# Seven products of halves for eight in 18 of 22 projection steps, and the splits of their weights on ScalarE and VectorE

## What is computed

```python
h    = rms_norm(x, norm_w)
proj = h @ w_in                       # 1024 x 1024 times 1024 x (all columns)
gq, gk, gv, g_low, gr, hq, hf, hi, hg, sz, sxbc, sdt, gates = split(proj)
...                                   # GLA, HGRN2 and Mamba-2 (conv over sxbc) give y, 2048 wide
x2   = x + merged(y, sigmoid(gates)) @ w_out
h2   = rms_norm(x2); route each token to 1 of 4 groups, 2 of 8 experts
out  = rms_norm(x2 + w1 * expert1(h2) + w2 * expert2(h2), final_w)
```

## Time and profile before

| | us |
|---|---|
| median of 3 runs | 2144.92 (2144.08 to 2148.81) |
| the profiled execution | 2143.66 |
| its span, first to last instruction | 2142.0 |
| mean granted TensorE clock | 0.971 of full speed |
| project, from its first product to the next block's first | 139.07 to 628.17 |
| mixers, from there to the merge's first product | 628.17 to 1163.89 |

### The profile page before, as it was taken

The page is one execution under the profiler, slowest core; times in us unless marked ns, Lnnn a source line. Parts: engine busy times, 40 slices in busy tenths (PEclk is TensorE's granted clock), DMA queues, the critical chain, the costliest instruction groups (busy, mean ns, idle before and its releaser), DMA issues. The chain is left out here.

```text
span 2142.0 us, 26814 instructions
## 1 busy us (share of the span) xinstructions
PE 1979.7 (92%) x10826; PEld 1621.3 (76%) x10827; DVE 1337.7 (62%) x1475; ACT 921.4 (43%) x998; POOL 362.7 (17%) x203
## 2 busy tenths in 40 slices
PE   6999999999999999999997999986699999999994
PEld 5778888888987777777775787865588888888872
DVE  5930000576215777877874565556698999999974
ACT  4211010112114444444443334231578888878863
POOL 4223232243310000000001000012122222222210
PEclk9999999999999999999998999998799999999997
DMA  5242222224236553565645754451799999999986
GB/s 160 82 157 98 99 98 79 78 79 137 80 103 151 151 165 120 147 157 161 149 121 187 258 216 162 154 206 60 293 367 382 386 391 384 388 386 388 386 328 247
DMA packets 217236, 435.97 MB, mean 204 GB/s; under 512 B 27730, under 2 KB 150754, under 8 KB 189602
## 3 DMA queue, kind: packets, MB, share of 16 engines
q1 hardware_dynamic: 185954, 361.97, 49.3%
q10 hardware_dynamic: 20288, 51.39, 6.7%
q0 software_dynamic: 10880, 21.03, 2.6%
HBM read 369.67 MB, written 81.43 MB: 211 GB/s over the span
## 5 line engine op out<-in xcount | busy, mean ns | idle before, releaser
L636 DVE TENSOR_SCALAR tap<-u,taps 128x1024 f32<-128x1024 f32 x16 | 20.1, 1297 | 293.1 <-ACT u L594 293.1
L666 PE MATMUL ps<-h_hi,w_hi 128*128 128x512 f32 x576 | 178.1, 391 | 2.4 <-PEq L58 2.4
L666 PE MATMUL ps<-h_hi,w_lo 128*128 128x512 f32 x576 | 177.8, 390 | 0.0
L666 PE MATMUL ps<-h_lo,w_hi 128*128 128x512 f32 x576 | 177.7, 390 | 0.0
L2416 DVE TENSOR_TENSOR gu_lo<-gate_raw,gu_hi 128x2048 fp32r<-128x2048 f32 x64 | 146.6, 2293 | 32.8 <-ACT gu_hi L2361 32.7
L1311 PE MATMUL psum<-h_hi,l_hi 128*128 128x512 f32 x384 | 158.7, 413 | 3.5 <-PEq L58 3.5
L1311 PE MATMUL psum<-h_lo,l_hi 128*128 128x512 f32 x384 | 160.1, 417 | 0.0
L1311 PE MATMUL psum<-h_hi,l_lo 128*128 128x512 f32 x384 | 157.5, 410 | 0.0
L2416 DVE TENSOR_TENSOR gu_lo<-up_raw,gu_hi 128x2048 fp32r<-128x2048 f32 x64 | 146.4, 2287 | 13.7 <-ACT gu_hi L2361 13.7
L2421 DVE TENSOR_TENSOR dn_lo<-dn_raw,dn_hi 128x2048 fp32r<-128x2048 f32 x62 | 142.0, 2292 | 16.4 <-ACT dn_hi L2371 13.2
L604 ACT ACTIVATE out<-ps 128x2048 f32<-128x2048 f32 x14 | 26.4, 1883 | 270.2 <-PE ps L666 201.2
(11 more groups left out here) (383 smaller groups left out, 4863.2 us busy)
## 6 DMA issues: line engine op xcount, KB each, us to landing
gate_raw<-moe SPq DMA_DIRECT2D x66, 1024.0 KB, 8.4
up_raw<-moe SPq DMA_DIRECT2D x64, 1024.0 KB, 8.1
dn_raw<-moe SPq DMA_DIRECT2D x62, 1024.0 KB, 7.5
w_raw<-w_in SPq DMA_DIRECT2D x26, 1024.0 KB, 6.3
dn_raw<-w_br SPq DMA_DIRECT2D x15, 1024.0 KB, 7.4
l_raw<-w_gates ACTq DMA_DIRECT2D x24, 512.0 KB, 6.0
s_gates<-l_out ACTq DMA_DIRECT2D x48, 256.0 KB, 4.4
gate<-s_gates SPq DMA_DIRECT2D x16, 768.0 KB, 5.6
```

What stands on the lines that cost most here:

```text
L666: ins = nc.tensor.matmul(ps[b][:, a * T + half * 512:a * T + half * 512 + 512], w[:, k, a * P:(a + 1) * P], h[:, k, half * 512:half * 512 ...
```

## The change

1. **project** runs as two tokens steps, then 18 row steps with silu and conv in turn (the last two are silu), then two tokens steps, unrolled. A row step has 7 groups of 12 matmuls of 512 columns (Strassen's scheme in Winograd's form, one level, over halves of the columns, of k and of the tokens). The tokens' sums of halves `th`, `tl` are built once at the start of the block on DVE and ACT. The weights' sums of halves (`summed`), the subtractions of the splits (`lower`) and three additions of results (`added`) are on DVE, the casts (`upper`) and copies out of PSUM on ACT; POOL has only the two tiles of the gates left. The first tap of a convolution moves to ACT. PE waits for ACT's copies before groups 2 and 4 and for DVE's addition before group 6, since they use the same PSUM banks again. Outputs go out as two transfers a step. `out[0]` is the gates' `l_raw`, so these are loaded at the end of the block.
2. **norm1_and_decays**: the transposes of chunks 1 and 3 go to a second PSUM tile, the casts of chunks 2 and 3 to ACT, chunk 4 is transposed after PE's first products have begun.
3. **ident** is built in each stage that uses it; in the mixers POOL builds it last.
4. `gates` and `y` are laid out in DRAM so that each partition reads 4 to 6 KB in a row.
5. **merge_and_route**: the work beside the second half comes one column tile later, DVE's order at its end changes, the records' constant fields are written ahead, the last places come before the last `h2`, the records are read before `work` is stored; this block and the experts' end without a drain of POOL.
6. **finish**: `ON_PE` is (2, 3, 5, 6).

```diff
 norm1_and_decays, ScalarE and TensorE
+                if c == NCH // 2:
+                    upper_part(2)
+                    upper_part(3)
...
-            TURNS = {(0, 4): NCH // 2 + 1, (1, 2): NCH // 2 + 2, (2, 0): NCH // 2 + 3}
+            TURNS = {(0, 2): NCH // 2, (0, 7): NCH // 2 + 1, (1, 4): NCH // 2 + 2, (2, 1): NCH // 2 + 3}
 project, ScalarE
+            def step(n):
+                b, before = n % 2, is_conv(n - 1)
+                act.wait_ge(group_done, G * n + 1)
...
+                nc.scalar.copy(place(n, 0, 0), X[b]).then_inc(snap_ready, 1)
+                upper(n + 1, 0)
+                act.wait_ge(group_done, G * n + 2)
+                nc.scalar.copy(place(n, 1, 1), Y[b]).then_inc(snap_ready, 1)
+                upper(n + 1, 1)
+                act.wait_ge(group_done, G * n + 3)
+                nc.scalar.copy(place(n, 0, 1), X[b]).then_inc(snap_ready, 1)
+                for g in (2, 3, 4):
+                    upper(n + 1, g)
+                if before:
+                    conv_out(n - 1, 0)
+                upper(n + 1, 5)
+                if not is_conv(n):
+                    act.wait_ge(c_ready, 3 * n + 3)
+                    nc.scalar.activation(row(n, 0), row(n, 0), ACT.Silu).then_inc(out_ready, 1)
+                    send(n, 0)
+                act.wait_ge(group_done, G * n + 7)
...
+                upper(n + 1, 6)
+                if is_conv(n):
+                    conv_first(n, 0)
+                    conv_first(n, 1)
+                else:
+                    nc.scalar.activation(place(n, 1, 1), place(n, 1, 1), ACT.Silu).then_inc(out_ready, 1)
+                    act.wait_ge(x_read, n + 1)
+                    send(n, 1)
+                if before:
+                    conv_out(n - 1, 1)
...
+            for n in range(N):
+                step(n)
+            tokens_hi(N + HEAD, 2)
+            act.wait_ge(c_ready, 3 * N)
+            tokens_hi(N + HEAD + 1, 3)
+            tokens_out(N + HEAD, 2)
 project, VectorE
+            def step(n):
+                m = n + 1
+                summed(m, 0)
+                tap(n - 1, 0, 1)
+                lower(m, 0)
+                tap(n - 1, 0, 2)
+                lower(m, 1)
+                summed(m, 1)
+                tap(n - 1, 0, 3)
+                lower(m, 2)
+                summed(m, 2)
+                tap(n - 1, 1, 1)
+                added(n, 0)
+                lower(m, 3)
+                tap(n - 1, 1, 2)
+                added(n, 1)
+                summed(m, 3)
+                lower(m, 4)
+                tap(n - 1, 1, 3)
+                added(n, 2)
+                lower(m, 5)
+                lower(m, 6)
 project, TensorE
+            def step(n):
+                b = n % 2
+                moving = (rows_of(0, 0), (th[0], tl[0]), (th[1], tl[1]), rows_of(1, 0), (th[2], tl[2]), rows_of(1, 1), (th[3], tl[3]))
+                for g, (bank, first) in enumerate(((X, True), (Y, True), (X, False), (Z, True), (X, False), (Y, False), (X, False))):
+                    pe.wait_ge(split_ready, G * n + g + 1)
...
+                    if g == 2:
+                        pe.wait_ge(snap_ready, 3 * n + 1)
+                    if g == 4:
+                        pe.wait_ge(snap_ready, 3 * n + 3)
+                    if g == 6:
+                        pe.wait_ge(c_ready, 3 * n + 2)
 mixers, GpSimd, VectorE and TensorE
             nc.gpsimd.memset(mean_b[:], 1.0 / 256).then_inc(const_ready, 1)
+            nc.gpsimd.memset(ident[:], 0.0).then_inc(ident0, 1)
+            pool.wait_ge(ident0, 1)
+            nc.gpsimd.affine_select(out=ident[:], in_=ident[:], compare_op=ALU.not_equal, fill=1.0, base=0,
+                                    pattern=[[-1, P]], channel_multiplier=1).then_inc(ident_ready, 1)
...
             dve.wait_ge(mask_ready, NL)
+            dve.wait_ge(ident_ready, 1)
...
             pe.wait_ge(tok_loaded, 32)
+            pe.wait_ge(ident_ready, 1)
 merge_and_route
-        block = ctx.enter_context(nc.Block())
+        block = ctx.enter_context(nc.Block(no_gpsimd_drain=True))
...
+    def beside(n):
+
+        return 2 <= n - DM < 2 + HC
...
             for n in range(DM, 2 * DM):
-                gated(n)
+                if n < 2 * DM - 1:
+                    gated(n)
                 rest_w(step_of(n) + 2)
...
+            gated(2 * DM - 1)
+            pick_second(0)
+            weights(0)
...
+            weights(3)
+            places(3)
             h2(HC + 3, 5)
-            places(3)
 finish
-    ON_PE = (1, 3, 4, 6)
+    ON_PE = (2, 3, 5, 6)
 the tensors in DRAM
-        ("gates", [3072, T], F32),
+        ("gates", [2, D // P, P, 3, T // 2], F32),
...
-        ("y", [2048, T], F32),
+        ("y", [2, P, 16, T // 2], F32),
```

More of the change, by code:

```diff
@@ L510, in project @@
         sem = semaphores(nc, ctx, qk_stored)
[L511 to L514, removed]
+        whole = lambda ap: ap.rearrange("p b k n -> p (b k n)")
+        tiled = lambda ap: whole(ap).rearrange("p (k t) -> p k t", t=S)
+        out = [whole(l_raw), sb("out1", [P, 2 * T])[:]]
+        th = [sb(f"th{i}", [P, KH, S], F32R) for i in range(3)] + [tiled(l_hi)]
@@ L529, in project, with block_of @@
         block = ctx.enter_context(nc.Block())
[L531 to L545, removed]
+        def block_of(n, i, j):
+            return w_raw[:, n % 2, j * KH:(j + 1) * KH, i * P:(i + 1) * P]
@@ new lines, in tap @@
+            def tap(n, a, k):
+                if not is_conv(n):
+                    return
+                if k == 1:
+                    dve.wait_ge(tap_ready, 2 * convs(n) + a + 1)
+                    if a == 0:
+                        dve.wait_ge(c_ready, 3 * n + 3)
+                    else:
+                        dve.wait_ge(x_read, n + 1)
+                ins = nc.vector.scalar_tensor_tensor(row(n, a), u[a][:, k:k + T], tap_col(n, a, k), row(n, a),
+                                                     ALU.mult, ALU.add)
+                if k < SSM_CONV - 1:
+                    own.link(ins)
+                else:
+                    ins.then_inc(conv_ready, 1)
@@ new lines, in _ @@
+            for b in range(2):
+                dve.wait_ge(qk_stored[b], 16 * 2)
+            rows(0)
+            tokens_split(1, 0)
+            rows_split(0)
+            for k in range(1, KH):
+                rows(k)
+                rows_split(k)
+            for a in range(2):
+                nc.vector.memset(u[a][:, 0:PAD], 0.0).then_inc(pad_ready, 1)
+            dve.wait_ge(pad_ready, 2)
+            summed(0, 0)
+            lower(0, 0)
+            lower(0, 1)
+            summed(0, 1)
@@ L670, in _, with tokens @@
-            steps(pe, body)
+            def tokens(t, i):
+                b = t % 2
+                if i:
+                    pe.wait_ge(tok_split, i)
+                if i >= 2:
+                    pe.wait_ge(x_read, N - 3 + i)
+                    pe.wait_ge(c_ready, 3 * (N - 3 + i))
+                parts = ((w_hi[:, b], h_hi), (w_hi[:, b], h_lo), (w_lo[:, b], h_hi))
+                for c in range(NCH):
+                    for k in range(KT):
+                        for n, (w, h) in enumerate(parts):
+                            ins = nc.tensor.matmul(ps[b][:, c * PAIR:(c + 1) * PAIR], h[:, k, c * CH:(c + 1) * CH], w[:, k, :],
+                                                   start=k == 0 and n == 0, stop=k == KT - 1 and n == 2)
+                ins.then_inc(tok_done, 1)
@@ L673 @@
+            tokens(0, 0)
+            tokens(1, 1)
+            for n in range(N):
+                step(n)
+            tokens(N + HEAD, 2)
+            tokens(N + HEAD + 1, 3)
 LATE_T = WIDTHS["gates"] // P
```

491 lines of the change are left out of this document (317 added, 174 removed).

## The result

The changed kernel takes 2125.1 us (median of 4 runs, 2123.06 to 2130.35), the kernel before 2145.88 beside it (4 runs): ratio 0.9906, interval 0.9884 to 0.9928. It is faster by 20.8 us, about 1%. I had forecast 2097 and a range of 2086 to 2117, so the sign is right and the size is less than half of what I gave.

What follows compares the result with a forecast made beforehand. PE was taken to bound the kernel, busy for 92% of the span. Terms −49.0 − 3.4 + 8 + 8.6 − 1.5 − 2.1 − 1.8 − 1.5 − 3.9 = −46.6 against 2143.66 gave 2097 us, range 2086 to 2117.

Steps and rivals of the forecast that it cites:

- The row steps: Projection: 18 steps each lose 12 of 96 matmuls, −49.0 us, 19.05 us a step with PE staying the bound.
- B: Projection: DVE or ACT misses its date in each silu/conv pair by 1 to 3 us, 2105 to 2121; chance 0.27.
- D: Projection: PE stops briefly at group 2 or 6 of every step and its clock falls each time, 2153; chance 0.04.
- E: Projection's head stalls too, combined tiles late by up to 5 us, 2102; chance 0.07.
- I take no stall: Row steps: DVE (slack 1.4 us) and ACT (slack 1.2) keep PE's pace; bounds none and 24 us.
- The tail: Projection's end: PE runs dry 5.9 us before the third tokens step, plus 2.1 for the clock; +8, bounds +4 to +9.
- The mixers: PE waits 8.1 us for POOL's identity, clock costs 2.5, later waits absorb some; +8.6, bounds +5 to +11.
- The merge: Longer DRAM runs speed loads, −1.5; in the second half the shift by one tile shortens waits, −2.1.
- The routing's −1.8: Routing's tail: records before `work` and places before `h2` save 1.8 us.
- The experts: Experts' end: leaving out POOL's drain shortens the 3.5 us to the next block; −1.5, bounds 0 and −2.5.
- The finish: DVE's wait of 3.94 us for PE's sum of chunk 1 goes, as chunks 0 and 1 become its own; −3.9.
- The head: norm1: first product near 24.4 instead of 27.86, with casts on ACT and no chunk 4 ahead; −3.4, bounds 0 and −5.

Runs made afterwards that it cites:

- e8: The changed kernel with four 128x512 subtractions on GpSimd added at the start of each of the 18 row steps, into an unread tile; 2152.76 us, one run.
- e3: The changed kernel with the last row step collecting results in the convolution's buffers u, its SiLU writing from there to the output buffer; 2116.64 us.
- e2: The changed kernel with the third tokens step's weights cast after group 3 of the last row step and subtracted in that step; 2118.22 us.
- e5: The changed kernel with the former order of the merge's second half: work one column tile earlier again, VectorE's former order; 2123.7 us.
- e7: The changed kernel with SyncE issuing the four transfers of h2 one column tile later, behind the next weights' load; 2124.29 us.
- e6: The changed kernel with VectorE making the output product's last two splits before the second pick and the first half's weights in the merge; 2122.71 us.
- e4: The changed kernel with the drain of GpSimd back at the ends of the merge's and the first slabs' blocks; 2120.29 us.
- e10: The changed kernel with the finish's sums on TensorE for chunks 1, 3, 4, 6 again; 2127.77 us, one run.
- e1: The changed kernel with GpSimd building the identity first instead of last in the mixers; 2114.65 us.

## Why the prediction was right and wrong

- **The row steps: right.** PE's 12 matmuls fewer in 18 steps came whole, and none of my rivals B, D and E occurred: no wait before groups 2, 4 or 6 in 17 steps, no low clock among them, no late first row step. The slack that I worked out for VectorE, 1.4 us, was too large. In the step that starts at 259.63 the second addition ends at 274.44 + 0.69 = 275.13, 15.5 us after the start where I had 14.9, and group 6 starts at 276.00: 0.9 us, and 1.1 by e8. The step held all the same, with less room than I gave it.

```profile
259.63 0.19 PEld L923 LDWEIGHTS ps<-h_hi,w_hi 128*128 128x128 f32 x1
...
274.44 0.69 DVE L814 TENSOR_TENSOR l_raw<-ps,l_raw 128x512 f32<-128x512 f32 x1
...
276.00 0.19 PEld L923 LDWEIGHTS ps<-l_hi,w_hi 128*128 128x128 f32 x1
```

One small term was missing: a step's pitch is 19.17 us and not 19.05 (starts at 240.45, 259.63 in the timeline of weight loads), as the 12 matmuls of group 6, with the tiles `l_hi` and `l_lo` as moving input, take 2.80 us where the other groups take 2.72, and the group after them 2.77. That is 2.2 us over 18 steps.
- **The projection's largest miss: a step that I never worked through.** I went through a silu step after a conv step and a conv step after a silu step, and took the last two for the same. The sentence that failed is "I take no stall". In step 17 the first copy's target is an output buffer, and its release is a transfer's landing: the copy starts 6.5 us behind that transfer's issue at the end of step 16 (519.76 − 513.27). e3 shows 8.3 us for it: 5.74 of stop, and for the rest the slow clock after it (0.60 in the 5 us from 520.50).
- **The tail: right** (+8 forecast, 8.3 by e2).
- **The mixers: mechanism and size right, the discount wrong.** Up to chunk 0's first wait they came out at +10.4 us where stop and clock were 8.1 + 2.5 in the prediction; the stop was 10.29, since PE ran the filling ahead of it at full clock this time and came 2.5 us sooner. That made the stop longer and nothing else later: it ends when POOL has the identity, 16.1 us after the block's start (610.71 − 594.57), and the same in e2 and e3, where PE came later and the stop was 8.75 and 8.76. I subtracted 2.0 for waits that I counted as absorbed; they stand at 0.52 and 1.43, as before the change.
- **The merge: the sign wrong.** The layouts gave nothing that the waits show (−1.5 forecast; no run changes them alone): after the first product PE waits in the first half for 2.42 + 0.85 + 2.78 + 0.94 = 6.99 us before and 0.83 + 0.91 + 0.88 + 3.54 + 0.67 = 6.83 now. For the second half I had −2.1. The wait for `h2T` did not go with the shift; it grew from 4.34 to 6.27 (3.87 without the shift, e5). The step that failed is that `h2T` "no longer stands behind the weights' cast": one tile later it stands behind the next cast, whose weights arrive late as well, half of it behind the transfers of h2 (e7). The wait at the output product went from 4.64 + 1.87 to 7.71, from the picks that the prediction named and priced too low (e6). The routing's −1.8 is there once the drain is back (18.25 us of waiting at the experts' first transpose in e4 against 20.37 before); in the changed kernel the block's longer end without the drain ate it (20.19).
- **The experts: the sign wrong.** I took the 3.5 us between two blocks for the price of the drain and gave −1.5. Without it they became 6.35 (e4). I had no row that showed a drain; a gain was the one end of the range that I should not have made the value.
- **The finish: right in kind** (e10); the new waits of 0.34 and 1.02 us for chunks 2 and 3 keep 1.3 of the 3.9 us.
- **The head: right by luck in part.** The first product comes at 25.66 in place of 27.86, −2.2, behind `va_lo`, not −3.4. The other 1.2 us are the clock's, which differs there between executions of the same code (last section): at the clock of the kernel before, 0.91, e4 and e5 reach the projection at 136.69 and 136.51, 2.4 to 2.6 us sooner than it, and the six profiles at 0.83 reach it at 139.4 to 139.8, no sooner at all. No run puts the head back alone.

In sum the forecast missed by 27 us: 10.8 in the projection, 7.2 in the merge, 5.3 in the experts' end, 2.3 in the mixers, 1.3 in the finish. The steps that failed are "I take no stall", which step 17 breaks (8.3 us); the shift and the picks in the merge, taken as a gain of 2.1; and the missing drain, taken as a gain of 1.5 (it cost 2.7 and 2.1 us in the two gaps). The range erred by the same habit: its bounds were made for each term, the one term that wasn't seen had none, and the drain's worst bound was 0.

## What to carry to other kernels

When a loop's steps are of several kinds, work through the step at each change of kind and the last one, buffer by buffer: a release by a transfer's landing (6 us here) hides in the one step that breaks the pattern. A constant that PE needs early is built first on its engine, and a new wait of PE in a fixed stream is worth its full length, in the projection with 2.5 us more for the slow clock behind it. Six such places, found in the traces and mended by a few lines each, gave 38.7 us together, where the change as a whole had given 20.8. And a pace that leaves VectorE about 1 us of slack in 19 held only as long as GpSimd kept still.

## What was not expected of the hardware

- A block's end without GpSimd's drain was longer than with it, 6.35 against 3.6 us at the experts' end and 4.8 against 2.7 us at the merge's, from SyncE's last issue to its next. Why stays open.
- The granted clock falls in stretches in which PE never stops. Between 80 and 100 us PE is busy for 20.00 of 20.00 us in all twelve profiles, and the clock there was 0.91 in three of them (before, e4, e5), 1.00 in three (the changed kernel, the first line, with e1 and e6) and 0.83 in six (e2, the second line, and the others). The code up to there is the same in all but the kernel before:

```profile
80.00:100.00 20.00, 20.00 (x81) 14.69 (x80) 19.19 (x12) 6.50 (x6) 7.48 (x2) 1.00 0.23 91
```

```profile
80.00:100.00 20.00, 20.00 (x67) 13.81 (x66) 19.16 (x13) 6.51 (x6) 7.42 (x2) 0.83 0.24 98
```

- With it the projection's first product lies between 135.5 and 139.8 us in profiles that share the code up to there, and the mixers' stage between 545.4 and 554.9 us in nine profiles of the same mixers. That is as much as the medians scatter, and the reason why a term of 3 us can only be read at milestones within one execution.
